# Where six bias loads stand among the reloads of cached memory keys and values, and how the last two weight fills of a mixture of experts are cut

## The reference, cut to what matters

```python
h = h + cross_attend(rms_norm(h, norm_x), mem_k, mem_v, w_xq, w_xo)   # 4 heads of 256, 256 memory tokens
h = h + moe_ffn(rms_norm(h, norm_ffn), ...)                           # top 4 of 32 experts

# cross attention: each of the 8 sample rows has its own cached keys and values, (256, 4, 256)
s = einsum('bthd,bmhd->bhtm', q, mem_k) * 256 ** -0.5
o = einsum('bhtm,bmhd->bthd', softmax(s), mem_v)

# one expert: w1 is 1024 x 2048, w2 is 1024 x 1024, b1 and b2 are added before and after
hh = xt @ w1 + b1
glu, lin = minimum(hh[:, 0::2], 7), clip(hh[:, 1::2], -7, 7)
y = ((lin + 1) * (glu * sigmoid(1.702 * glu))) @ w2 + b2
acc = acc + gate * y
```

## Time and profile before

| What | us |
|---|---|
| median of 3 runs (lowest, highest) | 1498.06 (1497.56, 1500.62) |
| time of the profiled execution | 1499.03 |
| its span, first to last instruction | 1497.2 |
| PE busy | 1385.4 |
| DVE, ACT, POOL busy | 460.6, 238.2, 42.5 |

### The profile page before, as it was taken

One profiled execution on the slowest core, in us unless ns is written; L12 is line 12 of the kernel. 1 busy time (PEld: TensorE's weight loads), 2 busy tenths in 40 slices (PEclk: granted clock), 3 DMA queues, 4 the chain that ended last, 5 costly groups with the idle time before them and its releaser, 6 DMA issues.

```text
span 1497.2 us, 21274 instructions
## 1 busy us (share of the span) xinstructions
PE 1385.4 (93%) x8579; PEld 685.2 (46%) x8579; DVE 460.6 (31%) x1116; ACT 238.2 (16%) x428; POOL 42.5 (3%) x37
## 2 busy tenths in 40 slices
PE   8999899899998989999998989989989899899896
PEld 7667776554486453333333333333333333333332
DVE  1856643553024252122122112211221131122213
ACT  1053322321012440000000000100000001011002
POOL 0000111000000320000000000000000000000000
PEclk9999999999999999999999999999999999999999
DMA  9111534438365649999999999999999999999996
GB/s 366 39 37 74 198 143 148 184 151 328 141 253 172 237 191 422 425 426 424 427 424 424 427 425 425 427 424 426 426 423 428 424 424 427 424 426 426 424 427 244
DMA packets 96724, 490.69 MB, mean 328 GB/s; under 512 B 9307, under 2 KB 14527, under 8 KB 61626
## 3 DMA queue, kind: packets, MB, share of 16 engines
q1 hardware_dynamic: 94074, 468.89, 76.4%
q0 software_dynamic: 2304, 20.97, 3.6%
q10 hardware_dynamic: 296, 0.11, 0.0%
HBM read 484.01 MB, written 6.04 MB: 327 GB/s over the span
## 4 chain that ended last, share of the span: by engine, by line
PE 41%; DMA 17%; DVE 6%; issue 2%; SPq 1%; ACT 1%; POOL 1%; DVEq 0%
DMA arena<-in_w_e 16%; PE ps L1985 15%; PE ps L2021 15%; PE ps L2033 4%; PE ps L1975 2%; PE ps L2008 2%; DVE arena L2545 1%; DVE arena L2555 1%; DVE arena L2552 1%; DVE arena L2553 1%; PE ps L2049 1%; PE ps L2063 1%; SPq L1459 1%; DMA arena<-in_cache_mem_k 1%; PE ps L2037 1%
## 5 line engine op out<-in xcount | busy, mean ns | idle before, releaser
L1985 PE MATMUL ps<-arena 128*64 128x512 f32 x2048 | 454.5, 595 | 18.0 <-DMA arena<-in_w_e 17.4
L1985 PEld LDWEIGHTS ps<-arena 128*64 128x64 f32 x2048 | 145.3, 137 | 299.2 <-issue 297.7
L2021 PE MATMUL ps<-arena 128*64 128x512 f32 x960 | 226.1, 631 | 2.1 <-ACT arena L2233 2.1
L2021 PEld LDWEIGHTS ps<-arena 128*64 128x64 f32 x960 | 78.4, 147 | 147.8 <-issue 134.9
L2552 DVE TENSOR_SCALAR arena<-ps 128x1024 f32<-128x1024 f32 x15 | 18.4, 1224 | 292.3 <-PE ps L1985 292.3
L2564 DVE COPY arena<-ps 128x512 f32<-128x512 f32 x15 | 10.4, 691 | 228.5 <-PE ps L2021 228.5
L2231 ACT ACTIVATE arena<-arena 128x1024 f32<-128x1024 f32 x15 | 15.9, 1058 | 324.3 <-DVE arena L2552 324.3
L2570 DVE TENSOR_TENSOR res<-res,ps 128x512 f32<-128x512 f32 x60 | 41.2, 687 | 81.1 <-PE ps L2033 81.1
L2008 PE MATMUL ps<-cst,arena 128*128 128x128 f32 x120 | 22.8, 352 | 43.7 <-DVE arena L2545 43.7
L1968 PEld LDWEIGHTS ps<-arena 128*128 128x128 bf16 x768 | 49.4, 99 | 14.2 <-issue 12.2
L1742 PE MATMUL ps<-arena 128*128 128x512 f32 x128 | 55.8, 594 | 0.0
(11 more groups left out here) (552 smaller groups left out, 1532.7 us busy)
## 6 DMA issues: line engine op xcount, KB each, us to landing
arena<-in_w_e SPq DMA_DIRECT2D x384, 1024.0 KB, 17.8
arena<-in_w_in SPq DMA_DIRECT2D x8, 1380.0 KB, 17.8
arena<-in_cache_mem_k SPq DMA_DIRECT2D x8, 1024.0 KB, 8.7
arena<-in_w_out SPq DMA_DIRECT2D x2, 2048.0 KB
arena<-in_w_xk SPq DMA_DIRECT2D x1, 4096.0 KB, 16.2
arena<-in_w_xv SPq DMA_DIRECT2D x1, 4096.0 KB, 13.7
arena<-in_w_xq SPq DMA_DIRECT2D x1, 4096.0 KB, 23.0
arena<-in_cache_mem_v SPq DMA_DIRECT2D x1, 4096.0 KB, 16.2
```

The source lines that it names most:

```text
L1985: last = pe.matmul(ps[64 * x:64 * x + 64, c, :], xe[:, k, 64 * x:64 * x + 64], ring[n % RING][:, c * 512:(c + 1) * 512], start=False, stop ...
L2021: last = pe.matmul(ps[64 * x:64 * x + 64, 4 + c, :], aT[:, k, 64 * x:64 * x + 64], ring[(n + x) % RING][:, j * D + c * 512:j * D + (c + 1) ...
```

## The change

Two edits. In the SP list the six bias loads move from behind the key reloads of b = 1, 2, 3 to places ahead of the value reloads of b = 0, 1, 2, and the wait for the stores (`stored`) moves behind the four key reloads. And the last two fills of the last pair are cut the other way: instead of one fill for each expert with k steps 6 and 7, one fill for each k step with both experts. PE's last 16 matmuls keep their number, order and shapes; they wait for the first of the two fills, do k step 6, then wait for the second.

```diff
+    def fill_both(sp, k, place, landed):
+        src = w_e2[0, NE - 2:NE, k * P:(k + 1) * P, :].rearrange("x p n -> p x n")
+        sp.dma_start(place.rearrange("p (x n) -> p x n", x=2), src).then_inc(landed, 16)
...
             fill(sp, 3, 0)
-            sp.wait_ge(stored, memory_stored)
             for b in range(G):
                 sp.wait_ge(sx["scored"], b + 1)
                 sp.dma_start(Kx[:, b], cache_mem_k[0, G + b].rearrange("(s p) h n -> p s (h n)", p=P)).then_inc(kx_loaded[b], 16)
-                if b > 0:
-                    part = slice((b - 1) * NE, b * NE)
+            sp.wait_ge(stored, memory_stored)
+            for b in range(G):
+                if b < XPARTS:
+                    part = slice(b * NE, (b + 1) * NE)
                     sp.dma_start(bias[part, 0:2 * D], b_e1[0]).then_inc(mo["b_loaded"], 16)
                     sp.dma_start(bias[part, 2 * D:3 * D], b_e2[0]).then_inc(mo["b_loaded"], 16)
-            for b in range(G):
                 sp.wait_ge(sx["scored"], G + b + 1)
                 sp.dma_start(Kx[:, b], cache_mem_v[0, G + b].rearrange("(s p) h n -> p s (h n)", p=P)).then_inc(kx_loaded[b], 16)
...
-            for n in range(RING, FILLS):
+            for n in range(RING, FILLS - 2):
                 sp.wait_ge(free[n % RING], final * 2 + 1)
                 fill(sp, n, NE - 2)
+            for j in range(2):
+                n = FILLS - 2 + j
+                sp.wait_ge(free[n % RING], final * 2 + 1)
+                fill_both(sp, KD - 2 + j, ring[n % RING], full[n % RING])
...
+            def last_two(it, n):
+                for j in range(2):
+                    pe.wait_ge(full[(n + j) % RING], (it * 2 + (n + j) // RING + 1) * 16)
+                    for c in range(2):
+                        for x in range(2):
+                            last = pe.matmul(ps[64 * x:64 * x + 64, 4 + c, :], aT[:, KD - 2 + j, 64 * x:64 * x + 64],
+                                             ring[(n + j) % RING][:, x * D + c * 512:x * D + (c + 1) * 512],
+                                             start=False, stop=(j == 1), skip_group_check=True)
+                    last.then_inc(free[(n + j) % RING], 1)
...
-            last_output(final, 22)
+            last_two(final, 22)
```

## The result

| | median us | runs | ratio to before, 95% interval |
|---|---|---|---|
| before, in the same launches | 1499.55 | 20 | |
| changed | 1503.42 | 20 | 1.0022 (1.0011 to 1.0032) |

The change makes the kernel slower, by 3.3 us (1.6 to 4.8). The forecast was 1.7 us faster, with 0.62 on no difference and 0.08 on slower; the time lies outside its range. The profiled execution has a span of 1502.4 us, 5.2 above that of before.

The account below looks back on a forecast made before the run. The prediction took the experts' weight stream through the DMA engines as the bound; its start comes 0.4 us earlier (2.1 - 1.7) and the end gains 1.3, 1.7 in all: 1496.4 us, range for 8 in 10 1493.0 to 1498.6.

Parts of the forecast that it names:

- Edit 1, the keys: Key reloads without biases: both PE waits (1.31 and 1.96 us) go, last scores start 5.1 us earlier.
- Edit 1, the biases: Bias loads between values: last pair lands at 494.9, so ACT's cast starts 2.1 us earlier than 497.04.
- 3 x 2.65 + 2 x 2.4: Queue behind the last keys: three bias pairs at 2.65 us and two value loads at 2.4, added to 482.2.
- a rival, in a stronger form: Last bias pair lands behind the values, near 500; PE idles 8 us; 4.6 us slower, 1502.7; chance 0.06.
- What that does to PE: PE idles 3.3 us before the second transposes, then runs at low clock; 1.7 us lost, stream starts 0.4 earlier.
- I take 1.7: Cost of low clock behind PE's new wait, 1.7 us, from 1.2 to 2.5 in the experts' loop.
- The upper bound written down, 2.9: Most the low clock behind PE's new wait could cost: half of the 5.8 us at 819.64 in the experts' loop.
- Edit 2: At the kernel's end, last fills cut by k step: PE's idle gap closes, gain 1.28 us.
- The sum: Whole kernel: 0.4 us at the stream's start plus 1.3 at the end, 1.7 us faster.
- The slow fills: New last fills read two rows 4 MiB apart and take twice as long; 3.2 us slower, 1501.3; chance 0.03.
- The clock did not stay up: Rival that full clock holds behind PE's new wait; 3.4 us faster, 1494.7; chance 0.13.
- The biases in time by 492: Bias pairs cost little outside the keys' traffic and land by 492; 6.4 us faster, 1491.7; chance 0.12.

Follow-up runs that it names:

- clock_kept: bias_first with 7 unread 128x256 matmuls in each of two 1.9 us PE waits ahead of the first expert matmuls; ratio to before 0.9948.
- clock_kept_4: clock_kept with 4 instead of 7 unread matmuls in each of the two PE waits; ratio to before 0.9952.
- wide_first: gap_short and bias_first_gap, each with wide projections ahead of the narrow router logits; one run each, 90.7 and 96.6 us from block start to experts.
- values_held: The changed kernel with the last two value reloads and the router's loads held until all six bias loads landed; ratio to before 0.9997.
- gap_short: bias_first with one more 2.75 us ACT cast ahead of the biases' signal, so PE idles 3.0 us; ratio to before 0.9996.
- wide_first_long: bias_first_gap with the wide projections ahead of the narrow router logits; one run, second transposes to sample rows' matmuls 9.1 us instead of 11.4.
- pe_busy_6: The changed kernel with 6 unread 128x512 matmuls in PE's wait before the second group of output transposes; ratio to before 0.9990.
- moved_only: The kernel before with only the bias loads moved, its last fills as they were; ratio to before 1.0014.
- cut_only: The kernel before with only the last two fills cut by k step, biases in their old place; ratio to before 0.9985.
- bias_first_gap: bias_first with two more 2.75 us ACT casts ahead of the biases' signal, so PE idles 5.8 us; ratio to before 1.0035.
- bias_first: The changed kernel with two bias pairs ahead of the keys, the third before the values, an early fill behind the router's loads; ratio to before 0.9961.
- pe_busy: The changed kernel with 12 unread 128x512 matmuls in PE's wait before the second group of output transposes; ratio to before 1.0018.

## Why the prediction was wrong, step by step

- **Edit 1, the keys.** The gain was right. Both waits went, and the last scores came 5.1 us earlier from the block's start, as reckoned. There was luck in it: the last keys landed 19.7 us after the block's start, later than the 18.0 to 19.3 forecast and only 0.1 us ahead of need; in clock_kept, clock_kept_4 and the two wide_first kernels they came too late.
- **Edit 1, the biases.** Mis-sized. The last landing was forecast at 494.9, 30.65 us after the block's start, and came at 33.1. The step that failed here is the term "3 x 2.65 + 2 x 2.4", which leaves out the loads issued behind the last pair. Of the 2.5 us, about 1.5 are those (values_held has 1 to 2); 1.0 was there already at the first pair (21.6 instead of 20.6), and its cause stays open. The prediction had the mechanism as a rival, in a stronger form (landing near 500), and gave it 0.06. Its time, 1502.7, is near the measured one partly by luck: it had the landing too late and the clock's price too low (2.9). In place of 2.1 us gained at the cast there were 0.4 lost, and PE's wait was 5.83 us, not 3.3.
- **What that does to PE.** The step that failed most: "I take 1.7" for the low clock. The stage lost 5.0 us. The price had been taken from the experts' loop, where a gap of 2.9 us cost 1.2 to 2.5. Two things differ: here the wait was 5.8 us, and transposes and narrow logits stand behind it; in the loop there are transposes and then wide matmuls. gap_short shows that the longer wait is not the main thing (3.0 us, 4.7 lost), and one execution of wide_first_long that the order of work behind it is worth 2.3. pe_busy_6 shows that the clock is the cause: with the wait filled the 5.0 us are gone. The upper bound written down, 2.9, was half of a low stretch of the loop and so no bound for another place. The prediction also said that a gap of 2.06 us was not followed by a slower clock; in moved_only it was.
- **Edit 2.** Right: 1.28 us of gap closed, and about 1.6 us less from the first expert matmuls to the end (941.5 to 939.9).
- **The sum.** Forecast 0.4 earlier at the experts, measured 6.1 later: cast 0.4, stage 5.0, and 0.7 behind the stage. The last is not shown to be the change's: it is mostly the last router logits, which ran at low clock (1.92 us for 1.08), but the same stretch took still longer in cut_only, where nothing ahead of it was edited (29.7 us; 29.3 after, 28.5 before). With edit 2, 6.1 - 1.6 = 4.5 us for this pair of executions, within the timed 3.3 (1.6 to 4.8).
- **The rivals.** The slow fills didn't occur (2.5 us apart, as before). The clock did not stay up. The biases in time by 492 did not occur either: the pairs cost more than reckoned, not less. In another place in the queue they were in time, and then the gain was 5.8 and 6.3 us, each give or take 2, near that rival's 6.4.

## What to carry to other kernels

When two engines arrive at a meeting point nearly together, making one of them earlier buys an idle time for it, and on PE that idle time can have a price of its own. Here five executions with a wait of 3.0 to 5.8 us lost another 4.4 to 5.2 us to the low clock, and the same work after a filled wait lost nothing. Don't take the price of a low clock from another stage, where other work stands behind the wait, and ask whether independent wide work can be moved into it. A load that gates a serial chain on another engine belongs ahead of the bulk loads that nobody waits for yet: putting the same six loads in front of the first value reload, instead of between the reloads, turned 0.2% slower into 0.4% faster.

## What the runs showed of the hardware that was not expected

- The granted clock stayed at 0.50 through 10 us of uninterrupted PE work behind one wait (changed, moved_only, bias_first_gap: stage 11.2 to 11.4 us for 6.2), and for more than 9 us behind a wait of 3.0 (gap_short).
- Waits of one length do not always have one outcome. The experts' loop has 15 gaps of 2.9 us in each of the sixteen profiles; 226 of the 240 were followed within 2.2 us by a granted clock of 0.50, 14 were not. The wait of 2.06 us at the block's start was followed by it in one profile of sixteen.
- A load of 32 rows lands later when other loads are issued behind it in the same queue: 13.3 us to landing, 11.5 with those held back (one execution; 9.8 us between first and last pair, 10.7 to 11.8 in the five with the loads behind).
- Two loads of 256 and 128 KiB to 32 partitions cost 1.7 us among themselves (bias_first), 2.6 to 3.7 between loads of 1 MiB.
- A float32 matmul of 128x512 with 128 columns of weights is two records and 0.86 us at full clock (pe_busy), of 128x256 0.43 us (clock_kept), from start to start.
